# Scan of an RWKV-7 layer: keys and values turned to time-major order by quadrants of 64 rows with a 64-column identity

## The chip, the cores and the metric

The kernel is one program on one core of a Trainium2 chip. The metric is the device time of one execution in microseconds (us). TensorE multiplies, VectorE (DVE), ScalarE (ACT) and GpSimd (POOL) work element by element, SyncE (SP) issues most DMA transfers. Matmul results land in PSUM, eight banks of 128 partitions x 512 fp32. The engines run on their own and wait for each other by semaphores.

## What is computed

Two two-layer transformer blocks in a row: differential attention and SwiGLU, then an RWKV-7 time mixer and a mixture of experts; after that MLA with retention, a conv-FFN, gated linear attention and again a conv-FFN. The model width is 1024, the sequence 256 tokens (272 with 16 meta tokens in the first block), all in fp32. The change lies in the RWKV-7 mixer, whose core is a recurrence over time, run forward and in reverse, with 16 heads of 64 channels:

```python
def _wkv7_step(S, inp):
    r, w, k, v, kk, a = inp
    sa = jnp.einsum('bhvk,bhk->bhv', S, kk)
    S = S * w[:, :, None, :] - sa[..., None] * (kk * a)[:, :, None, :] + v[..., None] * k[:, :, None, :]
    y = jnp.einsum('bhvk,bhk->bhv', S, r)
    return S, y
...
    _, y_fwd = lax.scan(_wkv7_step, S0, (r_t, tm(decay[0]), tm(kd[0]), v_t, kk_t, tm(a[0])))
    _, y_bwd = lax.scan(_wkv7_step, S0, (r_t, tm(decay[1]), tm(kd[1]), v_t, kk_t, tm(a[1])), reverse=True)
    y = jnp.swapaxes(y_fwd + y_bwd, 0, 1)
```

## The kernel before

Each engine has its own program, written as Python functions in stages: attention, ffn, project, scan, out, router, experts, even, conv, odd, conv. Activations are channel-major: 8 tiles of 128 channels (i = 0 to 7) by time. A tile holds two heads, head p = 0 in partitions 0 to 63 and p = 1 in 64 to 127.

**The scan.** The recurrence is cut into chunks of C = 64 time steps. Direction 0 has a first chunk of C0 = 16 and four of 64, direction 1 has four of 64: nine units (n, ci). The state of direction 0 lies in the buffer that the traces call `ring`, that of direction 1 in `arena`. scan_pe, scan_act and scan_dve each hold a generator `steps(n)` for a direction and `bonus()` for side work. The function `streams` runs them in turn, one step of direction 0, one of direction 1, one of the bonus work, in the same pattern on each engine. So the order on each engine is fixed. Direction 0 leads by some steps; a warm-up of matmuls (L591) fills a gap ahead of direction 1.

**One unit on TensorE.** In order: G, the products of keys with queries within the chunk, for each half of the tiles (q = 0, 1) 16 pairs of 64x64 by 128 (L1425); after the half q = 0 the values are turned to time-major order (Vt, L1434); then Ut (L1440), 64x64 by 64; then both key tensors are turned (BKt, L1447). After that come up to five levels lv of an inverse by doubling: T (L1454), Y (L1463) and X (L1469), 64x64 by 32 each. Then Z (L1475 and, with the state, L1483), N (L1489), the new state S (L1507) and the output y (L1500, L1515). `for i, p in HEADS` goes over tiles 0, 4, 1, 5, 2, 6, 3, 7 with p = 0 and 1 in each. The stationary operand comes first in `e.matmul(out, stationary, moving)`. `own(p)` is the partition half of head p. `part(j, i)` is the half j XOR (i // 4), so that tiles 0 to 3 and 4 to 7 land in opposite halves. So consecutive matmuls of L1440 go to four quadrants of the array in turn.

**Turning.** A transposition is a matmul with the window of 64 time steps as stationary operand and an identity as moving operand. Before, it takes a whole tile: 128 rows by 64 columns against the 128x128 identity `con("ident")`, with both heads next to each other in 128 output columns. Two tiles in turn use the two column halves of the array (TILES).

**Evictions.** ScalarE copies Vt to d.NV with two instructions (L1588), each 64 partitions by 512, scaled by a mask of real rows, and BKt to d.BKt in one (L1595, 128x1024). N is copied by the same kind of pair (L1612) from two banks of four blocks. VectorE masks G (L1706) and fills Y and X by predicated copies (L1713, L1720, L1728, L1732). TensorE waits for Vt before Z and for BKt before S.

**PSUM.** `psum.take(key, n)` hands out banks in turn; for n = 2 it takes an even bank and the next, skipping an odd one. A new holder waits until the old one is evicted.

**The identities.** `sn("id2")` is a 128x64 constant that already lies in SBUF with the scan's constants: two 64x64 identities, one above the other. After the scan, the weight stream goes on: the transfer of the block that begins with "rw_o" waits for the last y of direction 0 (L3580).

Of the kernel before, what the change touches and what calls it, by code (L numbers as in the profile page):

```python
# [416 lines left out]
def build(nc, x_d, ws_d, par_d, con_d, dis_d, scn_d, rel_d, ow_d, moe_d, pos_d, out_d):  # L417
    fp32, i32, u32, f32r = mybir.dt.float32, mybir.dt.int32, mybir.dt.uint32, mybir.dt.float32r
    ALU, ACT, AX = mybir.AluOpType, mybir.ActivationFunctionType, mybir.AxisListType
    MUL, ADD, SUB, MAXO, MINO = ALU.mult, ALU.add, ALU.subtract, ALU.max, ALU.min  # L420
    ctx = ExitStack()
    with ctx:
# [38 lines left out]
        PS = ps_t[:, :, :]  # L461
# [4 lines left out]
        def con(n):  # L466
            return con_t[:, cc[n][0]:cc[n][0] + cc[n][1]]
# [21 lines left out]
        pe, dv, ac, po = (Signal(sem(f"s_{n}_done")) for n in ("pe", "dve", "act", "pool"))  # L489
# [8 lines left out]
        psum = Banks()  # L498
# [585 lines left out]
        Rr, Kr, KK, Vr, Yb = (at(i * AB, 8, T0) for i in range(5))  # L1084
# [187 lines left out]
        def sn(name):  # L1272
            return scn[:, sc[name][0]:sc[name][0] + sc[name][1]]
# [33 lines left out]
        HEADS = [(i + 4 * x, p) for i in range(4) for x in range(2) for p in range(2)]  # L1307
        STRAIGHT = [(i, p) for i in range(8) for p in range(2)]
        SAME = [(i, p) for i, p in HEADS if i // 4 != p]
        OTHER = [(i, p) for i, p in HEADS if i // 4 == p]  # L1310
        TILES = [i + 4 * x for i in range(4) for x in range(2)]

        def own(p, n=64):
            return slice(64 * p, 64 * p + n)

        def part(j, i, n=64):
            return own(j ^ (i // 4), n)
# [7 lines left out]
        def bank(b, i):  # L1325
            return b + i // 4

        def col(i, n=64):
            return slice(64 * (i % 4), 64 * (i % 4) + n)
# [58 lines left out]
        def window(d, j, i, c0):  # L1388
            a = j * AB + i * T0 + c0
            return d.flat[:, a:a + 64]  # L1390

        def scan_pe(w, e):
            w.wait_ge(ac["project"], IN_SCN)

            def steps(n):
                d = dirs[n]
                for hf in range(2):
                    for name, src in (("w2", HW), ("a2", HA)):
                        for i in range(4):
                            b, free = psum.take((name, n, hf, i))  # L1400
# [11 lines left out]
                for ci, (c0, cn) in enumerate(d.chunks):  # L1412
                    u = (n, ci)
                    cs = slice(c0, c0 + cn)

                    for q in range(2):
                        b, free = psum.take(("G", *u, q), 2)
                        w.wait_ge(*free)
                        for i, p in HEADS:
                            if i // 2 % 2 == q:  # L1420
                                x = 128 * (g_slot(i, p) % 4)
                                for j in range(2):
                                    out = PS[part(j, i), b + p, x:x + 2 * C].rearrange("s (r t) -> s r t", r=2)
                                    if cn == C:
                                        last = e.matmul(out, window(d, j, i, c0)[own(p)], d.AR[own(p), :, i, cs], start=True, stop=True)  # L1425
                                    else:
                                        last = e.matmul(out[:, 0, 0:cn], window(d, j, i, c0)[own(p)], d.AR[own(p), 0, i, cs], start=True, stop=True)
                        last.then_inc(*pe.on("G", *u, q))
                        if q == 0:
                            b, free = psum.take(("Vt", *u))  # L1430
                            w.wait_ge(*free)
                            for i in TILES:
                                x = 128 * (i % 4)
                                last = e.matmul(PS[part(1, i), b, x:x + 128], Vr[:, i, c0:c0 + 64], con("ident"), start=True, stop=True)  # L1434
                            last.then_inc(*pe.on("Vt", *u))
                        yield
                    b, free = psum.take(("Ut", *u), 2)
# [4 lines left out]
                    b, free = psum.take(("BKt", *u), 2)  # L1442
                    w.wait_ge(*free)
                    for j in range(2):
                        for i in TILES:
                            x = 128 * (i % 4)
                            last = e.matmul(PS[part(j, i), bank(b, i), x:x + 128], window(d, j, i, c0), con("ident"), start=True, stop=True)  # L1447
                    last.then_inc(*pe.on("BKt", *u))
                    yield
                    for lv in range(1, levels(cn)):  # L1450
# [96 lines left out]
        def scan_act(w, e):  # L1547
            w.wait_ge(IN_SCN, IN_PAR)

            def steps(n):  # L1550
# [32 lines left out]
                for ci, (c0, cn) in enumerate(d.chunks):  # L1583
                    u = (n, ci)
                    w.wait_ge(pe["Vt", *u])
                    real = sn("rows")[:, int(cn < C):int(cn < C) + 1]
                    for x in range(2):
                        e.activation(d.NV[own(1 - x), 8 * x:8 * x + 8, :].rearrange("q i t -> q (i t)"), PS[own(1 - x), psum["Vt", *u], :], ACT.Identity, scale=real[own(1 - x)]).then_inc(*ac.on())  # L1588
                    ac.mark("Vt", *u)
                    psum.gone["Vt", *u] = [ac.now()]  # L1590
                    yield
                    yield
                    w.wait_ge(pe["BKt", *u])
                    b = psum["BKt", *u]
                    e.activation(d.BKt.rearrange("q (x i) p t -> q x (i p t)", x=2), PS[:, b:b + 2, :], ACT.Copy).then_inc(*ac.on("BKt", *u))  # L1595
                    psum.gone["BKt", *u] = [ac.now()]
                    yield
                    for lv in range(1, levels(cn)):
                        w.wait_ge(pe["T", *u, lv])
                        b = psum["T", *u, lv]  # L1600
                        e.activation(side(d.T.rearrange("q (x i) t -> q x (i t)", x=2), lv, d.y_side), PS[:, b:b + 2, 0:128].rearrange("q x (i m) -> q x i m", m=2 ** lv), ACT.Copy).then_inc(*ac.on("T", *u, lv))
                        psum.gone["T", *u, lv] = [ac.now()]
                        yield
                        yield
                    w.wait_ge(pe["Z", *u])
                    e.activation(pairs(d.Z), eights(psum["Z", *u]), ACT.Copy).then_inc(*ac.on("Z", *u))
                    psum.gone["Z", *u] = [ac.now()]
                    yield
                    w.wait_ge(pe["N", *u])
                    b = psum["N", *u]  # L1610
                    for x in range(2):
                        e.activation(d.NV[own(x), 8 * x:8 * x + 8, :].rearrange("q (i p) t -> q p i t", p=2), PS[own(x), b:b + 2, 0:256].rearrange("q p (i t) -> q p i t", i=4), ACT.Identity, scale=real[own(x)]).then_inc(*ac.on())  # L1612
                    ac.mark("N", *u)
                    psum.gone["N", *u] = [ac.now()]
                    yield
                    if ci < d.last:
                        identity(ci + 1)
                        yield
                    if cn < C:
                        continue  # L1620
                    if y_first(n, c0):
                        w.wait_ge(pe["y", *u])
                        e.activation(pairs(Yb[:, :, c0:c0 + cn]), eights(psum["y", *u], cn), ACT.Copy).then_inc(*ac.on("y", c0))
                        psum.gone["y", *u] = [ac.now()]
                    yield
# [2043 lines left out]
```

## Time and profile before

| | |
|---|---|
| median of 3 runs | 2608.56 us (2607.54 to 2610.41) |
| span of the profiled execution | 2600.0 us |
| median less span (start, end, spread) | 8.56 us |
| instructions on all engines | 54,588 |
| TensorE matmul rows | 23,472, busy 2505.0 us (96%) |
| VectorE | busy 1998.4 us (77%) |
| ScalarE | busy 1537.2 us (59%) |
| the scan | about 559 to 795 us of the span |

The profile is of one execution. Its own time is given as the span, from the first to the last instruction; the runs' times also hold what lies around it. A row names the line, the engine, the operation, output<-input by the program's names, partitions x elements, and how many. TensorE has two kinds of rows, PE (matmul) and PEld (weight load). One fp32 matmul of the code shows as two matmul rows and two weight loads. "issue" is time in which an engine waited for nothing that the profile shows. PEclk is the clock that TensorE was granted, as a share of 2.4 GHz.

### The profile page before, as it was taken

To read this page: it belongs to the slowest core of one execution; us is meant where nothing else is said; L and a number is where in the kernel's file an instruction comes from. 1 tells how busy PE (TensorE), PEld (TensorE's weight loads), DVE (VectorE), ACT (ScalarE), POOL (GpSimd) and SP (SyncE) were. 2 spreads that over 40 slices of the span, in tenths; PEclk is the share of its full clock that TensorE was granted. 3 is DMA by queue.
4 is the path that set the end of the run, shared out by engine and by line. 5 is a ranking of instruction groups with operands and counts; after the bars stand their busy time and mean duration, and the time that the engine had idled before them with its cause. 6 is when DMAs were issued, how large, how long until landed. Compare 5 with 4: busy or idle time off the path is not lost.

```text
span 2600.0 us, 54588 instructions
## 1 busy us (share of the span) xinstructions
PE 2505.0 (96%) x23472; PEld 2331.7 (90%) x23472; DVE 1998.4 (77%) x3066; ACT 1537.2 (59%) x2510; POOL 51.9 (2%) x57
## 2 busy tenths in 40 slices
PE   8999999989999999999999999999898899999999
PEld 8779998868887899999999999999897799998999
DVE  5555547775544799999999999999877788675884
ACT  4435434464432677777777777777666566564663
POOL 0001100000000000000000000000003000000000
PEclk9999999978999999999999999999999999998999
DMA  6223452300003599999999999999732255541453
GB/s 246 73 74 122 178 190 100 107 1 4 20 4 115 206 376 337 367 340 368 341 366 335 372 337 370 335 373 345 287 139 105 78 192 191 188 173 50 171 181 128
DMA packets 83257, 538.46 MB, mean 207 GB/s; under 512 B 9488, under 2 KB 9616, under 8 KB 38976
## 3 DMA queue, kind: packets, MB, share of 16 engines
q1 hardware_dynamic: 82368, 530.68, 55.2%
q8 instruction: 186, 3.05, 0.5%
q0 software_dynamic: 640, 4.22, 0.4%
q14 instruction: 63, 0.52, 0.1%
HBM read 533.81 MB, written 1.05 MB: 206 GB/s over the span
## 4 chain that ended last, share of the span: by engine, by line
PE 87%; DVE 7%; ACT 4%; issue 1%; DMA 1%; DVEq 0%; SPq 0%; PEldq 0%; ACTq 0%
PE ps L576 23%; PE ps L577 23%; PE ps L578 23%; PE ps L1469 2%; DVE sl L534 2%; PE ps L591 1%; PE ps L582 1%; PE ps L2000 1%; PE ps L1463 1%; PE ps L1447 1%; PE ps L1454 1%; DMA ring<-ws_d 1%; PE ps L2145 1%; PE ps L1425 1%; PE ps L819 1%
## 5 line engine op out<-in xcount | busy, mean ns | idle before, releaser
L2227 DVE TENSOR_TENSOR sl<-ring,sh 128x1024 fp32r<-128x1024 f32 x613 | 718.1, 1219 | 13.5 <-ACT sh L2185 10.6
L2185 ACT ACTIVATE sh<-ring 128x1024 fp32r<-128x1024 f32 x613 | 609.0, 1061 | 1.3 <-DVE xl L2070 1.3
L576 PE MATMUL ps<-sh,xh 128*128 128x256 f32 (+2 forms) x2012 | 568.0, 282 | 2.1 <-DVE sl L534 1.2
L578 PE MATMUL ps<-sh,xl 128*128 128x256 f32 (+2 forms) x2012 | 567.5, 282 | 0.0
L577 PE MATMUL ps<-sl,xh 128*128 128x256 f32 (+2 forms) x2012 | 567.0, 282 | 0.0
L576 PE MATMUL ps<-xh,sh 128*128 128x256 f32 (+2 forms) x1856 | 538.5, 290 | 22.8 <-DVE sl L534 12.7
L577 PE MATMUL ps<-xl,sh 128*128 128x256 f32 (+2 forms) x1856 | 531.2, 286 | 0.0
L578 PE MATMUL ps<-xh,sl 128*128 128x256 f32 (+2 forms) x1856 | 529.0, 285 | 0.0
L534 DVE TENSOR_TENSOR sl<-ring,sh 128x1024 fp32r<-128x1024 f32 (+1 forms) x341 | 401.0, 1201 | 74.6 <-ACT sh L527 74.3
L527 ACT ACTIVATE sh<-ring 128x1024 fp32r<-128x1024 f32 (+1 forms) x341 | 338.8, 1021 | 111.2 <-PE ps L578 102.8
L576 PEld LDWEIGHTS ps<-sh,xh 128*128 128x128 f32 x2012 | 377.8, 188 | 11.8 <-DVE sl L534 1.6
L577 PEld LDWEIGHTS ps<-sl,xh 128*128 128x128 f32 x2012 | 377.8, 188 | 8.9
L576 PEld LDWEIGHTS ps<-xh,sh 128*128 128x128 f32 (+1 forms) x1856 | 353.3, 190 | 32.6 <-DVE sl L534 12.2
L578 PEld LDWEIGHTS ps<-sh,xl 128*128 128x128 f32 x2012 | 377.8, 188 | 0.3
L578 PEld LDWEIGHTS ps<-xh,sl 128*128 128x128 f32 (+1 forms) x1856 | 354.2, 191 | 0.0
L577 PEld LDWEIGHTS ps<-xl,sh 128*128 128x128 f32 (+1 forms) x1856 | 353.6, 191 | 0.6
L2199 ACT ACTIVATE arena_moe<-ps 128x128 f32<-128x128 f32 x224 | 62.3, 278 | 245.1 <-PE ps L578 244.9
L576 PE MATMUL ps<-sh,moe_h 128*128 128x512 f32 x336 | 145.8, 434 | 1.9 <-DVE kept_l L2232 1.9
L577 PE MATMUL ps<-sl,moe_h 128*128 128x512 f32 x336 | 131.9, 393 | 0.0
L578 PE MATMUL ps<-sh,moe_l 128*128 128x512 f32 x336 | 131.8, 392 | 0.0
L578 PE MATMUL ps<-conv_h,sl 128*128 128x256 f32 x352 | 99.3, 282 | 0.0
L577 PE MATMUL ps<-conv_l,sh 128*128 128x256 f32 x352 | 98.6, 280 | 0.0
(555 smaller groups left out, 3861.1 us busy)
## 6 DMA issues: line engine op xcount, KB each, us to landing
ring<-ws_d SPq DMA_DIRECT2D x229, 1024.0 KB, 7.2
ring<-ws_d SPq DMA_DIRECT2D x80, 1536.0 KB, 6.4
ring<-ws_d SPq DMA_DIRECT2D x225, 512.0 KB, 6.5
ring<-ws_d SPq DMA_DIRECT2D x24, 1408.0 KB, 6.0
ring<-ws_d SPq DMA_DIRECT2D x4, 1256.0 KB, 5.4
ring<-ws_d SPq DMA_DIRECT2D x2, 1088.0 KB, 5.0
scan_t<-scn_d POOLq DMA_DIRECT2D x1, 1844.0 KB, 7.5
ring<-ws_d SPq DMA_DIRECT2D x1, 1248.0 KB, 5.6
```

Source lines behind the costliest of these rows:

```text
L527: e.activation(sh[slot_of[bi]][:, c], ring[:, bi % RING, c], ACT.Copy).then_inc(*ac.on("high", bi, p))
L534: e.tensor_tensor(sl[s][:, c], ring[:, bi % RING, c], f32(sh[s][:, c]), SUB).then_inc(*dv.on("low", bi, p))
L576: e.matmul(out, ah, bh, start=start, stop=False)
L577: e.matmul(out, ah, bl, start=False, stop=False)
L578: return e.matmul(out, al, bh, start=False, stop=stop)
L582: return e.transpose(out, in_, con("ident")[0:k, 0:k])
L591: e.matmul(PS[:, b, 0:256], con("o1024"), con_t[:, WARM:WARM + 256], start=True, stop=True)
L819: e.matmul(PS[:, b, 0:256], v, aT[h % 2][0:kn, kt, :], start=kt == 0, stop=False)
L1469: last = e.matmul(spread(PS[own(p), b:b + 2, :], lv)[:, i], d.T[own(p, cn), i, :], side(d.X[own(p, cn), i, :], lv, d.x_side), start=True, ...
L2185: e.activation(out, raw(u)[:, a:z], ACT.Copy).then_inc(*af.on("high", u, i))
L2199: e.activation(sg_few[u % 2][:, 0, :], PS[:, u % 2, 0:128], ACT.Sigmoid).then_inc(*af.on("sigmoid", u))
L2227: e.tensor_tensor(l, raw(u)[:, a:z], f32(h), SUB).then_inc(s_fd if i < 2 else s_fp, 1)
```

## The change

Values: the 8 matmuls of 128x64 by 128 become 16 of 64x64 by 64, one for each head, with the half of the 64-column identity that lies on the head's partitions. Their output now takes two PSUM banks, one for each p, of which 256 columns each are used; before it was one bank of 512. Keys: the 16 matmuls of the two key tensors become 32 of the same small form, in the same two banks but ordered by head. ScalarE's copies read and write the new order; their sizes stay as they were. TILES goes.

```diff
--- before.py
+++ after.py
@@ -1308,7 +1308,6 @@
         STRAIGHT = [(i, p) for i in range(8) for p in range(2)]
         SAME = [(i, p) for i, p in HEADS if i // 4 != p]
         OTHER = [(i, p) for i, p in HEADS if i // 4 == p]
-        TILES = [i + 4 * x for i in range(4) for x in range(2)]
 
         def own(p, n=64):
             return slice(64 * p, 64 * p + n)
@@ -1427,11 +1426,10 @@
                                         last = e.matmul(out[:, 0, 0:cn], window(d, j, i, c0)[own(p)], d.AR[own(p), 0, i, cs], start=True, stop=True)
                         last.then_inc(*pe.on("G", *u, q))
                         if q == 0:
-                            b, free = psum.take(("Vt", *u))
+                            b, free = psum.take(("Vt", *u), 2)
                             w.wait_ge(*free)
-                            for i in TILES:
-                                x = 128 * (i % 4)
-                                last = e.matmul(PS[part(1, i), b, x:x + 128], Vr[:, i, c0:c0 + 64], con("ident"), start=True, stop=True)
+                            for i, p in HEADS:
+                                last = e.matmul(PS[part(1, i), b + p, col(i)], Vr[own(p), i, c0:c0 + 64], sn("id2")[own(p)], start=True, stop=True)
                             last.then_inc(*pe.on("Vt", *u))
                         yield
                     b, free = psum.take(("Ut", *u), 2)
@@ -1442,9 +1440,8 @@
                     b, free = psum.take(("BKt", *u), 2)
                     w.wait_ge(*free)
                     for j in range(2):
-                        for i in TILES:
-                            x = 128 * (i % 4)
-                            last = e.matmul(PS[part(j, i), bank(b, i), x:x + 128], window(d, j, i, c0), con("ident"), start=True, stop=True)
+                        for i, p in HEADS:
+                            last = e.matmul(PS[part(j, i), b + p, 64 * i:64 * i + 64], window(d, j, i, c0)[own(p)], sn("id2")[own(p)], start=True, stop=True)
                     last.then_inc(*pe.on("BKt", *u))
                     yield
                     for lv in range(1, levels(cn)):
@@ -1584,15 +1581,16 @@
                     u = (n, ci)
                     w.wait_ge(pe["Vt", *u])
                     real = sn("rows")[:, int(cn < C):int(cn < C) + 1]
+                    b = psum["Vt", *u]
                     for x in range(2):
-                        e.activation(d.NV[own(1 - x), 8 * x:8 * x + 8, :].rearrange("q i t -> q (i t)"), PS[own(1 - x), psum["Vt", *u], :], ACT.Identity, scale=real[own(1 - x)]).then_inc(*ac.on())
+                        e.activation(d.NV[own(1 - x), 8 * x:8 * x + 8, :].rearrange("q (i p) t -> q p i t", p=2), PS[own(1 - x), b:b + 2, 0:256].rearrange("q p (i t) -> q p i t", i=4), ACT.Identity, scale=real[own(1 - x)]).then_inc(*ac.on())
                     ac.mark("Vt", *u)
                     psum.gone["Vt", *u] = [ac.now()]
                     yield
                     yield
                     w.wait_ge(pe["BKt", *u])
                     b = psum["BKt", *u]
-                    e.activation(d.BKt.rearrange("q (x i) p t -> q x (i p t)", x=2), PS[:, b:b + 2, :], ACT.Copy).then_inc(*ac.on("BKt", *u))
+                    e.activation(d.BKt.rearrange("q i p t -> q p i t"), PS[:, b:b + 2, :].rearrange("q p (i t) -> q p i t", i=8), ACT.Copy).then_inc(*ac.on("BKt", *u))
                     psum.gone["BKt", *u] = [ac.now()]
                     yield
                     for lv in range(1, levels(cn)):
```

## Rows read from the trace of the kernel before

**Rows 1.** The page: busy time by engine, and the instruction queue (packets, MB, share).
```profile
PE 2505.0 (96%) x23472; PEld 2331.7 (90%) x23472; DVE 1998.4 (77%) x3066; ACT 1537.2 (59%) x2510; POOL 51.9 (2%) x57
...
q8 instruction: 186, 3.05, 0.5%
```

**Rows 2.** Stretches: busy us (instructions) of each engine, granted clock, DMA share, GB/s.
```profile
559.00:586.00 27.00, 20.86 (x279) 16.66 (x277) 22.49 (x32) 14.71 (x23) 0.00 (x0) 0.75 0.01 2
586.00:600.00 14.00, 11.10 (x311) 9.40 (x311) 7.83 (x14) 6.84 (x12) 0.00 (x0) 0.88 0.01 4
601.00:615.00 14.00, 14.00 (x309) 11.97 (x310) 4.89 (x10) 5.13 (x10) 0.00 (x0) 0.51 0.01 4
615.00:767.00 152.00, 144.60 (x5100) 129.58 (x5092) 81.52 (x148) 59.50 (x109) 0.53 (x1) 1.00 0.04 11
670.00:751.00 81.00, 75.35 (x2826) 69.54 (x2820) 39.86 (x71) 30.07 (x53) 0.53 (x1) 1.00 0.06 17
1200.00:1500.00 300.00, 300.00 (x2192) 282.04 (x2191) 291.61 (x420) 226.72 (x348) 0.00 (x0) 1.00 0.96 356
```

**Rows 3.** Chain of waits, 713 to 752 us: start, duration, engine and line, count.
```profile
713.34 0.59 PE ps L1447 x8
713.93 0.48 issue
714.41 1.53 PE ps L1447 x24
...
718.09 0.59 PE ps L1454 x25
718.68 0.47 PE ps L1463 x32
...
721.85 0.59 PE ps L1454 x25
...
724.48 0.95 issue
725.43 0.83 PE ps L1469 x22
...
729.17 0.97 PE ps L1507 x25
...
730.75 0.93 PE ps L1469 x32
...
746.46 0.88 issue
```

**Rows 4.** DMA queues, 670 to 751 us: packets, MB, share of 16 engines.
```profile
q8 instruction: 22, 0.36, 1.9%
```

**Rows 5.** Order of time on TensorE, 618 to 650 us: start, us, instruction, count.
```profile
621.04 0.69 PE L1440 MATMUL ps<-scan_t 64*64 64x64 f32 x32
621.66 1.97 PE L1447 MATMUL ps<-con,scan_t 128*64 128x128 f32 x32
...
641.48 1.09 PE L1434 MATMUL ps<-con,arena 128*64 128x128 f32 x16
```

**Rows 6.** Chain of waits, 555 to 625 us, lines of the opening.
```profile
568.47 2.97 PE ps L1447 x31
...
587.29 1.05 PE ps L1434 x16
...
594.48 3.60 PE ps L1447 x31
...
609.04 1.01 PE ps L1463 x32
```

**Rows 7.** Order of time on ScalarE, 567 to 573 us; idle time before in brackets.
```profile
571.46 1.02 ACT L1595 ACTIVATE ring<-ps 128x1024 f32<-128x1024 f32 x1 [0.65 <-PE ps L1447]
```

**Rows 8.** Groups of the scan by form: count, busy us, mean ns, idle before.
```profile
L1588 ACT ACTIVATE ring<-ps,scan_t 64x512 f32<-64x512 f32 x10 | 6.8, 682 | 7.4 <-PE ps L1434 7.3
...
L1612 ACT ACTIVATE ring<-ps,scan_t 64x512 f32<-64x512 f32 x8 | 5.5, 682 | 6.9 <-PE ps L1489 6.8
```

## Prediction

> **What bounds the kernel now.** The first view is the page's head [rows 1]: TensorE is busy for 96% of the span of 2600.0 us. The change touches only the scan, so the second view is the table of stretches [rows 2]. It splits the scan in two. From 559 to 615 us the recurrences of the two directions start: TensorE, ScalarE and VectorE wait for one another, and TensorE's granted clock is at its lower level (1.2 GHz) for part of the time: 0.75, 0.88 and 0.51. From 615 to 767 us both directions run level by level, the clock is at its full 2.4 GHz and TensorE is busy for 144.60 of 152.00 us. One would say that it is TensorE-bound, and that whatever shortens a matmul shortens the kernel.
>
> The third view, the chain of waits, says otherwise [rows 3]. In 713 to 751 us it is nearly all TensorE, but with holes put down to "issue", as 0.48, 0.95 and 0.88 us. Nothing on another engine ends them. They fall inside a group of like matmuls: the one at 713.93 cuts the 32 of L1447 into 8 and 24, which have no wait between them. Work resumes at 714.41, 718.09, 721.85, 725.43 and 729.17 us, so 3.68, 3.76, 3.58 and 3.74 us apart, mean 3.69, whatever the line.
>
> The fourth view, the DMA queues, has the same period [rows 4]: from 670 to 751 us queue q8, of kind "instruction", moved 22 packets, one each 81.0/22 = 3.68 us. In that stretch TensorE ran 2826 matmuls and 2820 weight loads [rows 2], 5646/22 = 257 for each packet. On the page q8 has 186 packets in all and TensorE 46,944 such instructions [rows 1], 252 for each. So q8 brings TensorE its instructions in packets of 3.05 MB/186 = 16.4 KB; from 670 to 751 us TensorE eats them as fast as they come and stands idle in between. The bound there is the number of instructions, at 81.0 us/5646 = 14.3 ns each, and not the matmuls' time. In all of 615 to 767 us it is 152.0/10,192 = 14.9 ns each, so within 4% of that rate.
>
> **The change, part by part.** (1) TensorE's time. The keys and values of one chunk and direction (a unit; there are nine) take 8 matmuls for Vt and 16 for BKt, with a stationary operand of 128x64 and 128 moving columns. The trace shows each fp32 matmul as two matmul rows and two weight loads: from first start to last end 16 rows take 1.09 us, 32 take 1.97 us and L1440's 32 take 0.69 us [rows 5]. The next group starts 0.07 us before that end (621.04 + 0.69 against 621.66), so they hold the engine for 1.02, 1.90 and 0.62 us. After the change there are 32 and 64 rows of 64x64 by 64. The nearest row is L1440, with the same order over heads, the same quadrants (rows by p, columns by i // 4), the same two banks and the same 64 columns: 32 rows in 0.62 us, with a change of array shape before and after it. L1463, with its neighbours in the same shape, takes 0.47 us for 32 rows [rows 3]. I take 0.5 us for Vt and 1.0 us for BKt, since they now stand among matmuls of their own shape. That is 1.02 + 1.90 - 1.5 = 1.4 us less TensorE time in each unit, 12.8 us in nine; with 0.62 for each 32 it would be 1.06 us, 9.5 in all.
>
> On this the Trainium skill has two rules. The page "TensorEngine Tiling (Array Packing)", section "Tiling Modes", says that a 64x64 mode has four independent tiles and that a change of mode drains the array. The second agrees with the longer L1440, and both promise the gain in full, which is rival B below. The page "TensorE: Matmul & The Clock Gate", section "Wait — 56ns, not 53.3ns?", has a floor of about 25 ns from one matmul to the next however few the columns. By it the 96 rows of a unit would take 2.4 us and the gain would be 0.5 us. The trace has 0.62 us/32 = 19 ns for quadrant matmuls, so it does not bear the floor out here.
>
> (2) TensorE's instructions. Each added matmul brings two more matmul rows and two more weight loads. Vt goes from 32 to 64 instructions and BKt from 64 to 128: 96 more in each unit, 864 in the kernel, 864/257 = 3.4 more packets. This is what decides.
>
> Two of the nine units have their first Vt and BKt before 615 us (three of the four are in rows 6), so seven Vt and seven BKt lie from 615 to 767 us. That is 672 more instructions: 10,192 + 672 = 10,864. At the supply's 14.35 ns they need 155.9 us, 3.9 us more than the 152.0 of now. TensorE's own need falls by 7 x 1.4 = 9.8 us to 142 us, which is less than 155.9 and so buys nothing: it turns into longer holes. The price has bounds. With the shortest distance of two restarts, 3.58 us for 257 instructions or 13.9 ns, it is 151.3 us, 0.7 us less than now. With today's mean of this stretch, 14.9 ns, it is 162.0 us, a loss of 10.0 us. I take 14.35, as the stretch that has the holes is the one where supply alone sets the pace.
>
> (3) The opening, before 615 us. There supply is no bound: TensorE ran 622 instructions in the 14 us from 586 to 600 us [rows 2], 22.5 ns each, and waits for others. Three of the transposes are on the chain [rows 6]. BKt of the first unit ends at 571.44, then ScalarE evicts it (L1595, at 571.46), and only then starts direction 1's exponentials. ScalarE had been idle for 0.65 us there [rows 7], and BKt, 2.97 us now and at the lower clock in part, comes down to about half of that, so it is ready before ScalarE is: 0.65 us is gained. Vt of direction 1's first unit (587.29, 1.05 us) is waited for by L1588: 0.5 us. BKt of the same unit takes 3.60 us, most of it at the lower clock, ahead of L1595; at half speed L1463 takes 1.01 us for 32 rows [rows 6], so 64 rows want 1.8 to 2.0 us: 1.6 us, from 1.0 (all of it at the full clock before and after) to 2.6 (lower clock before, full after). Sum 2.75 us, bounds 2.0 and 3.8. What is late next is the queue of ScalarE (L1595, L1636, L1601), which moves along with BKt. The first unit's Vt is not in the chain: nothing. The stretch from 601 to 615 us at clock 0.51 has no transpose in it.
>
> (4) ScalarE's evictions. Vt's two now read two banks of four blocks each in place of 512 contiguous columns. L1612 is exactly the new form and takes 682 ns against 682 of L1588 [rows 8]: nothing. BKt's still moves 128x1024, 1.02 us now [rows 7]; its output goes in runs of 64, as that of L1612. Nothing, with a bound of 0.1 us for either sign.
>
> (5) PSUM. Vt takes two banks in place of one. The next request (G of the other half, two banks, aligned) skipped the odd one anyway, unless a one-bank request of the bonus work came between. No new wait is expected; the bound is one eviction's 0.7 us now and then, in a stretch where supply has TensorE waiting anyway. No DMA, no queue and no other wait is moved.
>
> (6) After the scan all is shifted: the transfer for the next projection waits for its last y (sp_program, L3580), and everything later for that. The code behind starts 96 instructions off the old packet borders. From 1200 to 1500 us TensorE ran 4383 instructions in 300 us, 68 ns each [rows 2], so packet borders cost nothing there.
>
> Sum: +3.9 - 2.75 = +1.15 us on the span of 2600.0 us. The median shown is 8.56 us above that span, which I keep: 2608.56 + 1.15 = 2609.7. The coverage by holes is never perfect (a wait for ScalarE adds to a packet's time where it doesn't fall in with a hole), so I round up to 2610.
>
> **The rivals.** A, the forecast: supply takes the gain, 2610. Its own range goes from 13.9 ns with 3.8 us of opening (-0.7 - 3.8 = -4.5) to 14.6 ns with 2.0 us (158.6 us, +6.6 - 2.0 = +4.6): 2604 to 2613.
>
> B: TensorE's time decides. For it: 144.60 of 152.00 us are busy, the chain is TensorE's, and outside 670 to 751 us holes are few: 144.60 - 75.35 = 69.3 of 71 us are busy. Against it: the restarts at a fixed 3.7 us. It would need the next packet to be asked for earlier when TensorE eats faster. It gives -12.8 us, with some of it lost to waits for VectorE and ScalarE: 2596 to 2600.
>
> C, the other side: the supply doesn't keep 14.35 ns for the new mix. The packets bunch: a unit's Ut and BKt become 192 instructions in a row in about 1.5 us, and other stretches are slow in instructions (L1515, L1425, the wait for L1612), so these go at TensorE's pace and the dense ones at the supply's, and both lose. That is today's 14.9 ns kept in spite of shorter matmuls: 162.0 us, +10.0 - 2.75 = +7.3 us, 2616. For it speaks that 615 to 767 us has 14.9 and not 14.35 today. It ends over the 0.2% line from 14.75 ns on (10,864 x 14.75 = 160.2 us, +8.2 - 2.75 = +5.5).
>
> D: the clock. From 601 to 615 us the grant is 0.51 while TensorE is busy for all 14.00 us [rows 2]; what went before is a stretch with waits at 0.88. These 14 us cost some 7. If the shift of 3 us or the thinner work before it moves that fall away, the gain is up to 7 us, 2603; if another such stretch comes, as holes grow, the loss is the same, 2617.
>
> E: the change doesn't do what it says, the quadrants not overlapping: L1469, whose blocks lie on the diagonal alone, needs 0.93 us for 32 rows [rows 3], and 96 rows at that pace 2.8 us, today's time. Then the opening gains nothing and supply still adds 3.9: 2612.5.
>
> **How the numbers follow.** A 0.50, B 0.12, C 0.20, D 0.13 (0.07 on the slow side, 0.06 on the fast), E 0.05. A measurement of this kernel tells about 0.2%, 5.2 us, from no change. Faster by more: B and most of D's fast side, 0.17. Slower by more: C and D's slow side, 0.27. Within: A and E, 0.56. The range leaves out B and the far ends of C and D: 2602 to 2618.
>
> **What the profile of after would show.** Right: rows of Vt and BKt at 0.5 and 1.0 us where they are not cut by a hole; q8 packets spaced at 3.6 to 3.8 us all through 615 to 770 us, 10,864/257 = 42 in place of 40, and 189 or 190 in all; more and longer "issue" holes, TensorE not busy for some 20 us of that stretch against 7.4; the scan's end within 3 us of now. Wrong: q8 packets nearer than 3.4 us (B), or a q8 mean above 3.8 us (C); a clock under 1.00 after 615 us, or over 0.6 from 601 to 615 (D); 32 rows of Vt in 0.9 us (E). If L1595 takes over 1.1 us, step 4 was wrong.

## The result, and the profile after

| | before | after |
|---|---|---|
| median of 6 runs each, taken in turn on one chip | 2608.05 us (2602.03 to 2612.46) | 2618.88 us (2615.99 to 2622.20) |
| ratio, 95% interval | | 1.0046 (1.0032 to 1.0061) |
| profiled execution, span | 2600.0 us | 2619.9 us |
| mean granted clock of TensorE over the run, mean of runs | 0.977 (109 runs, this study) | 0.971 (6 runs) |

The change makes the kernel 0.46% slower, 10.8 us. The forecast was 2610, its range ended at 2618.

The page of after, first the busy time by engine, then the instruction queue:

```profile
PE 2509.8 (96%) x23904; PEld 2332.2 (89%) x23904; DVE 1998.0 (76%) x3066; ACT 1536.9 (59%) x2510; POOL 51.8 (2%) x57
...
q8 instruction: 190, 3.11, 0.5%
```

There are 864 more TensorE instructions (47,808 for 46,944) and 190 packets for 186 [rows 1], as counted ahead. The stretches of after have the columns of [rows 2]; the last is new:

```profile
559.00:586.00 27.00, 18.59 (x325) 14.91 (x324) 22.55 (x33) 17.45 (x29) 0.00 (x0) 0.71 0.01 2
586.00:600.00 14.00, 11.71 (x345) 9.87 (x348) 10.92 (x16) 5.54 (x9) 0.00 (x0) 0.87 0.01 4
601.00:615.00 14.00, 13.75 (x282) 11.77 (x283) 4.53 (x9) 5.35 (x11) 0.00 (x0) 0.50 0.02 4
615.00:767.00 152.00, 131.56 (x5147) 120.01 (x5148) 76.45 (x139) 56.69 (x103) 0.53 (x1) 0.97 0.04 11
670.00:751.00 81.00, 67.38 (x2765) 62.28 (x2764) 39.73 (x72) 26.15 (x47) 0.53 (x1) 0.98 0.05 17
767.00:795.00 28.00, 25.96 (x573) 20.40 (x571) 8.62 (x16) 5.02 (x11) 0.00 (x0) 0.64 0.01 3
```

The same last stretch of before:

```profile
767.00:795.00 28.00, 25.61 (x750) 20.34 (x746) 8.79 (x19) 7.84 (x16) 0.00 (x0) 1.00 0.01 4
```

Two things are to be seen. From 615 to 767 us TensorE is busy for 131.56 us, not 144.60: it has less to do and does not get on faster. From 767 to 795 us it is busy as before, but the grant is 0.64, not 1.00, and it does 573 matmuls where it did 750. Its clock is at 1.2 GHz from 775.0 to 802.3 us.

The chain of waits of after shows both (start, duration, engine and line; L1444 is the new BKt, L1451, L1460 and L1466 are the old L1454, L1463 and L1469; L1535 and L1536 are the bonus work of the old L1538 and L1539):

```profile
719.60 1.01 issue
721.46 0.91 PE ps L1444 x64
722.68 1.85 issue
...
746.27 0.91 issue
749.58 1.17 issue
...
771.05 1.52 issue
773.00 0.93 PE ps L1466 x31
775.34 1.86 PE ps L1451 x64
777.20 1.20 PE ps L1535 x2
778.40 1.20 PE ps L1536 x2
779.61 1.01 PE ps L1460 x32
```

The holes put down to "issue" are longer than in [rows 3], up to 1.85 us where the longest was 0.95. Behind the last BKt comes one of 1.52 us. After 775 us every group takes nearly twice its time: L1460 1.01 us, where before's L1463 has 0.60 in the same stretch, L1535 1.20 where L1538 has 0.66. In before:

```profile
776.52 0.60 PE ps L1454 x32
...
779.38 0.66 PE ps L1538 x2
780.04 0.65 PE ps L1539 x2
780.69 0.60 PE ps L1463 x32
```

The scan's stages are split here by where groups start: G of direction 0, G of direction 1, G of the second unit of direction 0, the last G, the centering behind the scan. The low clock is the time at 1.2 GHz in that stage.

| us | before | after | after, second profile | low clock before / after / second |
|---|---|---|---|---|
| ahead of the scan (it starts at) | 560.0 | 563.7 | 563.2 | 34.1 / 41.0 / 41.0 |
| opening | 54.5 | 53.1 | 55.6 | 30.2 / 36.3 / 42.8 |
| main part | 142.4 | 150.2 | 147.1 | 0.5 / 8.1 / 8.4 |
| tail | 38.6 | 52.1 | 51.8 | 0 / 27.3 / 27.3 |
| behind the scan | 1804.5 | 1800.9 | 1808.0 | 42.8 / 42.7 / 56.4 |

The 19.9 us between the two spans are +3.7 ahead of the scan, -1.4, +7.8, +13.5 and -3.6 behind it. The parts outside the scan have the same code and move too: over the fifteen profiles of this study the scan starts at 558.4 to 566.0 us, and the part behind it takes 1800.8 to 1811.8 us. The tail is the one term that stands clear of this.

### The profile page after: what moved, and what is told of

Read it like the earlier page. It is cut to its first block, busy times and chain, and to the rows that moved or that the text cites. A ratio compares the mean times of both kernels' runs of the same rounds, so it can differ in the third digit from the quotient of the medians.

```text
span 2619.9 us, 55454 instructions
## 1 busy us (share of the span) xinstructions
PE 2509.8 (96%) x23904; PEld 2332.2 (89%) x23904; DVE 1998.0 (76%) x3066; ACT 1536.9 (59%) x2510; POOL 51.8 (2%) x57
## 3 DMA queue, kind: packets, MB, share of 16 engines
HBM read 533.81 MB, written 1.05 MB: 204 GB/s over the span
## 4 chain that ended last, share of the span: by engine, by line
PE 84%; DVE 9%; ACT 4%; issue 2%; DMA 1%; DVEq 0%; SPq 0%; PEldq 0%; ACTq 0%
PE ps L576 23%; PE ps L577 22%; PE ps L578 22%; DVE sl L534 2%; PE ps L1466 2%; PE ps L591 1%; PE ps L582 1%; PE ps L1998 1%; PE ps L1460 1%; PE ps L1451 1%; PE ps L819 1%; PE ps L1424 1%; ACT sh L527 1%; DMA ring<-ws_d 1%; PE ps L2143 1%
## 5 line engine op out<-in xcount | busy, mean ns | idle before, releaser
L2225 DVE TENSOR_TENSOR sl<-ring,sh 128x1024 fp32r<-128x1024 f32 x613 | 718.2, 1220 | 13.2 <-ACT sh L2183 10.5
L576 PEld LDWEIGHTS ps<-sh,xh 128*128 128x128 f32 x2012 | 377.7, 188 | 11.7 <-DVE sl L534 1.5
L576 PE MATMUL ps<-sh,moe_h 128*128 128x512 f32 x336 | 145.8, 434 | 1.9 <-DVE kept_l L2230 1.9
L576 PE MATMUL ps<-conv_h,sh 128*128 128x256 f32 x352 | 98.4, 279 | 0.8 <-DVE sl L534 0.8
```

Source lines behind the costliest of these rows:

```text
L576: e.matmul(out, ah, bh, start=start, stop=False)
L2225: e.tensor_tensor(l, raw(u)[:, a:z], f32(h), SUB).then_inc(s_fd if i < 2 else s_fp, 1)
```

## The experiments

All runs below are medians, with the kernel before run in turn on the same chip. Main part and tail are read as in the table above, from one profile each. The distance of packets is the mean from start to start of the packets of q8 that start in the main part. The main part of one profile is uncertain by some 3 us: nops96, which turned out to be a copy of before, has 145.8 for 142.4.

**after_again.** No edit: the changed kernel a second time.

> The changed kernel once more, beside the others. Theory S (instruction supply): in the profile the q8 packets stand 3.7 to 3.8 us apart from 622 us to the end of the units, 672 more instructions at 14.4 to 14.7 ns, +8 us there, -1 to -3 us in the opening. Theory D (clock) explains the rest of +10.8 us: lower-clock stretches of 20 to 27 us between the last unit's transposes and the end of the scan, worth 10 to 13 us; if the profile has no such stretch, the total is +5 to +7 us.

2619.73 us (2604.72 to 2632.61, 12 runs), ratio 1.0042 (1.0022 to 1.0063). The tail has the same 27.3 us at the low clock. The runs are spread widely and the spread goes with the clock: 2604.72 us at a mean grant of 0.977, 2632.61 us at 0.968. So the loss repeats, and the clock is in it.

**bkt_only and vt_only.** One half of the change each.

> Only the keys (BKt) by quadrants, the values as before: 576 more TensorE instructions, 448 of them in the supply-bound part. S: +448 x 14.4 ns = +6.5 us, less 1.5 us in the opening, +5 us. TensorE-time theory: 9 x 0.9 = -8 us. If the clock drops at the scan's end here too, up to 10 us more.

> Only the values (Vt) by quadrants, the keys as before: 288 more instructions, 224 of them in the supply-bound part. S: +3.2 us less 0.5 us in the opening, +2.7 us. TensorE-time theory: 9 x 0.5 = -4.5 us. Clock: less than with the keys.

```diff
 # bkt_only: BKt as after, Vt as before
-for i, p in HEADS:
-    last = e.matmul(PS[part(1, i), b + p, col(i)], Vr[own(p), i, c0:c0 + 64], sn("id2")[own(p)], ...)
+for i in TILES:
+    last = e.matmul(PS[part(1, i), b, x:x + 128], Vr[:, i, c0:c0 + 64], con("ident"), ...)
```

bkt_only: 2627.32 us (6 runs), ratio 1.0065 (1.0042 to 1.0087), main part 156.2 with 18.9 us at the low clock, tail 53.1 with 30.7. vt_only: 2604.68 us (12 runs), ratio 0.9992 (0.9977 to 1.0006), main part 143.0, tail 39.7 with none. The whole loss is BKt's. That bkt_only stands some 8 us above the changed kernel goes with the clock of its six runs: put to one grant both are at 2608 us (table of runs below). Vt alone costs nothing and gains nothing that can be told.

**nops96.** To the kernel before, 96 no-operations on TensorE in each unit.

> The kernel before with 96 TensorE no-operations after each unit's key transposes: as many instructions as the change adds (864), and no matmul touched. S: +672 x 14.4 ns = +9.7 us from 615 us on, and no gain in the opening, +10 us or a little more. TensorE-time theory: no-operations cost next to nothing, 0 to +2 us. Clock: TensorE's matmuls stay as thick as before in each unit but holes grow, so if holes alone bring the clock down, it falls here too.

2607.69 us, ratio 1.0004 (0.9991 to 1.0018), but with 186 packets: the no-operations left no instruction in the program. It tests nothing of supply, and stands as a control.

**half_keys and few_keys.** The kernel before with less TensorE time in BKt. In half_keys the moving operand has 64 of the 128 columns, so head 1 of each tile gets the turned keys of head 0; the count of instructions is kept. In few_keys tiles 4 to 7 are not turned but get those of tiles 0 to 3, which takes away 32 of BKt's 64 instructions. In both, ScalarE's copy of BKt reads each block twice, so that its output stays as large.

```diff
 # half_keys
-    last = e.matmul(PS[part(j, i), bank(b, i), x:x + 128], window(d, j, i, c0), con("ident"), ...)
+    last = e.matmul(PS[part(j, i), bank(b, i), x:x + 64], window(d, j, i, c0), con("ident")[:, 0:64], ...)
 # few_keys
-for i in TILES:
+for i in range(4):
```

> The kernel before with key transposes of 128x64 by 64 columns in place of 128: head 1 of each tile is left out of the transposes and gets head 0's keys. As many instructions as before, TensorE time of the key transposes about halved. TensorE-time theory: 9 x 0.8 = -7 us. S: the stretch from 615 us stays at 14.4 to 14.9 ns per instruction, gain only in the opening and the loose part, -2 to -4 us. D: thinner TensorE work alone brings the clock down at the scan's end, +8 to +14 us, with no instruction added.

> The kernel before with key transposes of tiles 0 to 3 alone (8 matmuls a unit in place of 16, 128x64 by 128 as before); tiles 4 to 7 are left out and get the keys of tiles 0 to 3. TensorE time of the key transposes is halved as in half_keys, but here with 32 instructions less a unit. S: 224 fewer in the supply-bound part, 3.2 us less than half_keys there, so -6 to -7 us on the kernel before. TensorE-time theory: the same as half_keys, -3.5 us.

Stretch 615 to 767 us of half_keys, columns as in [rows 2]:

```profile
615.00:767.00 152.00, 140.42 (x5102) 125.68 (x5100) 81.42 (x149) 59.71 (x109) 0.53 (x1) 1.00 0.04 11
```

The busy time falls from 144.60 to 140.42 us and the stretch holds the same 10,202 instructions (10,192 in [rows 2]); the main part is 142.6 us for 142.4, the total 2603.67 us, ratio 0.9991 (0.9980 to 1.0003). So in the main part shorter matmuls alone buy nothing that one profile can tell (the 4.2 us taken away are little more than the 3 us of nops96), which fits a pace set by the supply. The clock does not fall in the tail either, though BKt's matmuls are thin. few_keys: 2603.41 us, ratio 0.9987 (0.9972 to 1.0002), main part 144.2. Fewer instructions bring no more than shorter ones. The supply is not the only bound of the main part: its packets come 3.93 us apart for 3.82 in half_keys, and it is no faster. Part of that is its clock, which is low for 6.4 us of its main part, for 0.8 in half_keys.

**paired.** Keys interleaved by chunk in memory, so that one 128-column stationary operand holds both tensors: G becomes 64x128 and BKt 128x128 matmuls. That makes 192 matmul and weight-load rows in a full unit into 96, and what is computed stays the same; VectorE gets eight more, smaller operations, and ScalarE's decay factors wait for the keys.

```diff
-for j in range(2):
-    last = e.matmul(PS[part(j, i), bank(b, i), x:x + 128], window(d, j, i, c0), con("ident"), ...)
+last = e.matmul(PS[:, bank(b, i), x:x + 128], both(d, i, c0), con("ident"), ...)
```

> Fewer instructions, same results: the two key tensors lie next to each other by chunk, so that G takes 16 matmuls of 64x128 by 128 a unit in place of 32 of 64x64, and BKt 8 of 128x128 in place of 16 of 128x64. 96 TensorE instructions less in each of the eight full units, about as many as the change adds, with TensorE's streaming time near that of before; VectorE has 8 more small instructions in the opening, ScalarE none. S: 670 instructions less in the supply-bound part, -9.6 us until TensorE's own time takes over (it was busy for 144.6 of 152 us), so -5 to -7 us there, +1 us in the opening: -4 to -6 us in all, q8 at 182 or 183 packets. TensorE-time theory: 0 to +2 us. D: the clock stays up (all of the array in use more often).

Page and stretch of paired:

```profile
q8 instruction: 183, 3.00, 0.5%
...
615.00:767.00 152.00, 145.12 (x4689) 132.11 (x4686) 81.59 (x148) 58.12 (x105) 0.53 (x1) 0.98 0.04 11
```

2607.11 us, ratio 0.9996 (0.9981 to 1.0012). The gain of 4 to 6 us that I expected is not there. The packets now come 4.04 us apart on average in the main part (3.81 before), so supply no longer sets the pace; TensorE is busy for 145.12 us, as before. The reading that fits half_keys, few_keys and paired is that supply and TensorE's own work are level in the kernel before, so that taking from either alone gives nothing. It is argued, from one profile each.

**fill_after, wide and fill_tail.** The changed kernel with TensorE given thicker work. fill_after puts three idle matmuls of 128x128 by 256 ahead of each BKt, fill_tail ahead of the last unit's BKt of each direction only. wide lets 24 of the 32 matmuls of BKt have 128 moving columns (the extra 64 are overwritten by the next), with not one instruction more.

```diff
 # fill_tail (fill_after: in every unit)
+for _ in range(3 if ci == d.last else 0):
+    e.matmul(PS[:, b, 0:256], con("o1024"), con_t[:, WARM:WARM + 256], start=True, stop=True)
 # wide
-    last = e.matmul(PS[part(j, i), b + p, 64 * i:64 * i + 64], ..., sn("id2")[own(p)], ...)
+    last = e.matmul(PS[part(j, i), b + p, 64 * i:64 * i + wide], ..., eye, ...)
```

> The changed kernel with three filler matmuls of 128x128 by 256 ahead of each unit's key transposes (12 instructions and about 1.3 us of TensorE a unit, in the bank that the transposes then overwrite). Theory D (the clock falls because the quadrant form keeps too little of the array at work): the clock stays at 1.00 from 620 us to the scan's end, the tail is back at 39 us, and only the supply's price is left, +2 to +6 us on the kernel before. If the clock has nothing to do with what the matmuls fill, the 1.3 us a unit come on top: +11 to +20 us.

> The changed kernel with 128 moving columns in place of 64 for 24 of a unit's 32 key transposes (the surplus columns are overwritten by the next one): the same instructions as in the changed kernel, and TensorE time of the kernel before. S alone: as the changed kernel, +10 us, since holes take up the time. D, if streaming columns in quadrants is what counts: clock back to 1.00, +2 to +6 us. D, if rows of the array in use count (64 of 128): clock falls as in the changed kernel.

> The changed kernel with three filler matmuls of 128x128 by 256 ahead of the key transposes of the last unit of each direction only. D, with the fall decided by what stands just ahead of it: the lower-clock stretch of 27 us in the tail goes, the scan's tail is back to 39 to 41 us from 52, median +0 to +4 us on the kernel before. D, with the fall built up over all the units: the tail stays at 52 us and the median at +11 us or above.

The stretch that fell in after, here in fill_tail, then wide:

```profile
767.00:795.00 28.00, 27.05 (x829) 21.81 (x822) 11.93 (x22) 8.33 (x17) 0.00 (x0) 1.00 0.02 4
```

```profile
767.00:795.00 28.00, 26.16 (x834) 21.16 (x826) 12.14 (x23) 8.67 (x17) 0.00 (x0) 1.00 0.02 4
```

In all three the grant is 1.00 and the tail 40.3 or 40.4 us, for 52.1: 12 us are back, in the profiled execution. The totals gain less. fill_after 2616.04 us, ratio 1.0042 (1.0028 to 1.0056); wide 2613.30, 1.0037 (1.0019 to 1.0054); fill_tail 2614.22, 1.0024 (1.0011 to 1.0038). A filler of three takes 1.49 us in fill_tail, so six in fill_tail cost 3 us and the 27 of fill_after 13 us at the full clock if nothing hides them. The main part stays at 150.5 us in wide and in fill_tail and is 153.2 us in fill_after. So the fillers and the wider form bring back the tail, but the intervals of all three overlap with that of the changed kernel (1.0032 to 1.0061): that the total gains by them is not shown.

**vt_open.** vt_only with 12 filler matmuls, meant for the opening, to raise its clock. So that they can run while TensorE waits, the wait for T and X stands behind them. In the profile eight of them run in the opening and four at 623 and 631 us, in the main part.

```diff
+for _ in range(2 if u in ((0, 0), (1, 0)) else 0):
+    e.matmul(PS[:, b, 0:256], con("o1024"), con_t[:, WARM:WARM + 256], start=True, stop=True)
```

> Only the values by quadrants (as vt_only), and 12 filler matmuls of 128x128 by 256 in the waits of the first unit of each direction. If these lift the clock from 597 to 620 us, the opening loses most of its 30 to 40 us at the lower level, worth up to 10 us: -5 to -10 us. If not, the fillers cost up to 5 us where nothing hides them: 0 to +3 us.

2615.06 us, ratio 1.0030 (1.0013 to 1.0046). The opening still has 33.3 us at the low clock (vt_only 35.3) and is 57.0 us long for 54.6. The fillers buy no clock there. The 10 us above vt_only are not all theirs: in the two profiles the opening is 2.4 us longer and the main part 1.4, but the part behind the scan, whose code is the same, 7.4, with 59.7 us at the low clock for 45.9.

**keep_last and thin_tail.** Which units bring the fall? keep_last is the changed kernel with the old BKt in the last unit of each direction; thin_tail is the kernel before with the new BKt in these two units alone.

```diff
 # keep_last (thin_tail: the condition turned round)
+for i in (TILES if ci == d.last else []):
+    x = 128 * (i % 4)
+    last = e.matmul(PS[part(j, i), bank(b, i), x:x + 128], window(d, j, i, c0), con("ident"), ...)
-for i, p in HEADS:
+for i, p in ([] if ci == d.last else HEADS):
```

> The changed kernel, but the keys of the last unit of each direction are turned as before the change: 16 matmuls with 128 columns. The seven other units keep the quadrants; 128 TensorE instructions fewer than the changed kernel, so 189 or 190 packets. Theory L (the thin BKt of the last two units makes the clock fall near 775 us): the clock stays at 1.00 from 767 to 795 us, the way from the last G to the end of the scan is 38 to 41 us against 52, and the time is that of the changed kernel less 8 to 13 us: 2606 to 2611. Theory M (the fall comes from what went before, holes and thin work of the whole main part): the clock falls in the tail all the same, the tail takes 50 us or more, and the time is 2616 to 2622.

> The kernel before, but with the quadrant form of BKt in the last unit of each direction alone: 128 TensorE instructions more than before, 187 packets. Theory L (the last two units' thin BKt is enough): a fall of some 27 us in the tail at clock 1.2 GHz, tail 50 to 53 us, time 2617 to 2621. Theory M (it needs the holes of the main part, of which this kernel has few, about 9 to 13 us): no fall, tail 38 to 40 us, time 2605 to 2610.

Two stretches of keep_last:

```profile
615.00:767.00 152.00, 135.79 (x5046) 124.00 (x5042) 74.48 (x137) 56.37 (x102) 0.53 (x1) 0.92 0.04 11
767.00:795.00 28.00, 27.05 (x725) 20.72 (x717) 11.90 (x23) 8.08 (x17) 0.00 (x0) 1.00 0.01 4
```

and of thin_tail:

```profile
767.00:795.00 28.00, 27.35 (x771) 20.98 (x769) 9.58 (x20) 7.46 (x17) 0.00 (x0) 1.00 0.02 4
```

keep_last: 2613.76 us (2605.97 to 2616.82), ratio 1.0020 (1.0005 to 1.0034), tail 39.7 us with none at the low clock; but in its main part the clock fell for 20.5 us from 625.0 us on (grant 0.92), and that part took 153.6 us, 26.6 of them at the low clock. thin_tail: 2609.71 us (2602.45 to 2622.23), ratio 1.0017 (1.0000 to 1.0034), no fall in the profile; its slowest runs have the lowest clock (2622.23 us at 0.971, 2602.45 us at 0.980). So, as far as one profile each can tell, the fall in the tail goes with the new form in the last two units, but that form does not force it, which is neither theory in full. The ratios share the loss out: 0.17% for the two units alone, 0.20% for the seven others, 0.42 to 0.46% for all nine. The first two are barely clear of nothing.

**The hole behind the last BKt.** One more thing sets the kernels apart. In the three profiles with the long fall an "issue" hole starts within 0.5 us of the end of the last BKt and 2 to 4 us ahead of the fall: 1.52 us in after, 1.52 in after_again, 1.51 in bkt_only. In thin_tail it is

```profile
764.30 1.43 issue
```

and in wide 1.17 us, in vt_open 0.27, in fill_tail 0.18, in the other eight none; none of these falls. So where a hole of the supply lies goes along with the fall as well as the form of the matmuls does, and fillers or other counts of instructions move that too. No run holds one of the two and changes the other. A hole alone does not bring a long fall: after has one of 1.85 us at 722.68 and is low for only 3.4 us behind it, from 730.6 us.

**Time and clock, run by run.** Each run lists its span and the mean grant of TensorE's clock. Over 258 runs of 14 kernels, each against its own kernel's mean, the time goes up by 2.0 us for each 0.001 of mean grant lost, and what is left scatters by 2.6 us. A thousandth of 2610 us is 2.6 us of full clock, or 5.2 us spent at the half level. Put to a grant of 0.977 with that slope:

| kernel | runs | mean us | mean grant | us at 0.977 |
|---|---|---|---|---|
| before | 109 | 2607.6 | 0.9767 | 2607.0 |
| after and after_again | 18 | 2619.3 | 0.9714 | 2608 |
| bkt_only | 6 | 2624.8 | 0.9685 | 2608 |
| vt_only | 12 | 2604.5 | 0.9777 | 2606 |
| nops96 | 12 | 2607.8 | 0.9766 | 2607 |
| keep_last | 12 | 2612.4 | 0.9738 | 2606 |
| thin_tail | 12 | 2610.7 | 0.9757 | 2608 |
| fill_tail | 12 | 2614.6 | 0.9735 | 2608 |
| fill_after | 6 | 2617.4 | 0.9757 | 2615 |
| vt_open | 12 | 2614.9 | 0.9762 | 2613 |
| wide | 11 | 2616.0 | 0.9749 | 2612 |
| half_keys | 12 | 2603.7 | 0.9761 | 2602 |
| few_keys | 12 | 2604.7 | 0.9762 | 2603 |
| paired | 12 | 2607.9 | 0.9760 | 2606 |

At equal clock the changed kernel stands 1 us behind the one before. The other 10 or 11 us go with 0.005 of mean grant. This is a correlation, and fill_tail shows its limit. Its profile has no fall in the tail, and the grant of that same execution is still 0.974. The time at the low clock lies elsewhere: 51.2 us ahead of the scan, where before has 34.1 with the same code, and 8.6 in the main part, where before has 0.5. So a kernel's mean grant holds more than what its change does.

## Why the prediction was wrong

**What bounds the kernel: right in part.** half_keys takes 4 us of TensorE time out of the stretch with the number of instructions kept, and the main part does not move. But paired, with fewer instructions and the same TensorE time, does not move it either, so the number of instructions is not the only bound.

**(1) TensorE's time: right.** In the order of time of after, the new groups at full clock (start, us, instruction, count):

```profile
650.92 1.11 PE L1444 MATMUL ps<-scan_t 64*64 64x64 f32 x62
...
667.48 0.64 PE L1432 MATMUL ps<-scan_t,arena 64*64 64x64 f32 x32
```

The chain gives L1444 0.91 us for 64 rows (721.46), 1.0 was taken. L1432's next group starts 0.46 us after it (667.94), 0.5 was taken. Rival E is out.

**(2) The supply: right in kind, its size open.** +3.9 us was worked out, with 42 packets in place of 40 and some 20 us without work. TensorE is not busy for 20.4 us of 615 to 767 us. The main part has 40 packets for 38, on average 3.80 us apart for 3.81. It grew by 7.8 us, with 7.6 us more at the low clock. At half speed these cost 3.8 us at most, less where they fall in with holes: 4 us or more are left. In the second profile it is +4.7 and 7.9 us of low clock, 0.8 left. wide and fill_tail, with the same number of instructions or nearly, have +8.1 with 2.4 and with 8.1 us more of low clock. But nops96, the same program as before, has +3.4 with 1.3 more, vt_only, with a third of the added instructions, +0.6 with 1.8, and keep_last +11.2 with 26.1, less than half speed would make it. Whether the supply's price is 1 or 7 us can't be told from these profiles.

Rival B is out: the packets come no closer. (Its sign, packets nearer than 3.4 us, could not have told: single ones are 3.33 us apart in before as in after.) Rival C is not out. Its mechanism was today's mean rate kept in spite of shorter matmuls, and 3.80, 3.81 and 3.81 us for a packet in after, wide and fill_tail are today's 3.81; the forecast's 14.35 ns are 3.69 us for 257 instructions, and after_again comes nearest with 3.72. What speaks against C's +7.3 us in all is the 1 us that is left at equal clock.

**(3) The opening: too high.** -2.75 us was taken with bounds of 2.0 and 3.8. It is -1.4 and +1.1 us in the two profiles, each with more low clock than before (6.1 and 12.5 us). BKt of the first unit was no longer waited for, as ScalarE came to it straight from L1562 (start, us, instruction):

```profile
573.12 2.13 ACT L1562 ACTIVATE scan_t<-arena,scan_t,par 128x272 f32<-128x272 f32 x4
575.16 1.00 ACT L1593 ACTIVATE ring<-ps 128x1024 f32<-128x1024 f32 x1
```

But this piece gained nothing: L1593 is released 11.5 us behind the start of the scan, as before, since L1402 ahead of it held the chain for 3.14 us in place of 2.44 of its old line, L1403. The other two did shorten:

```profile
590.96 0.52 PE ps L1432 x31
...
597.62 1.75 PE ps L1444 x62
```

Vt of direction 1 has 0.52 us in place of 1.05, its BKt 1.75 in place of 3.60, together 2.4 us for the 2.1 taken. Behind them 1.0 us went again at the low clock. The step failed in keeping the clock of [rows 2] for the rest: the grant was 0.71 in place of 0.75 for the first 27 us. How much of that is the change's doing is open: nops96, the code of before, has an opening of 55.4 us.

**(4) The evictions: right.** L1586, the old L1588, is at 682 ns and L1593 at 1.00 us, against 682 ns and 1.02 us [rows 7, 8]. **(5) PSUM and (6) behind the scan** show no new wait in the chains; behind the scan the time goes -3.6 and +3.5 us, one way in one profile and the other way in the other.

**Where it went wrong: rival D.** Its slow side said 2617 us, near what was measured, with a chance of 0.07. (C's 2616 us is as near, and no better borne out.) I took the fall at 601 us [rows 2] as a single stretch that may move, be spared or come twice, 7 us each, by chance. What the runs show is that the kernels with the new BKt have a lower grant: 0.9714 and 0.9685 for 0.9767, over 18, 6 and 109 runs. The three profiled kernels that have it in all nine units with nothing thicker beside it (after, after_again, bkt_only) have 27.3, 27.3 and 30.7 us at the low clock in the tail, and 13.5, 13.2 and 14.5 us more tail. Of the profiles of the others none has that. Shorter matmuls without more instructions (half_keys) don't bring it, nor do as many instructions with wider ones (wide). But half_keys differs in more than the number, as it also keeps 128 rows of the array, and wide has a shorter hole behind its last BKt. TensorE is idle for 20.4 us of 615 to 767 us in after and for 11.6 in half_keys, which keeps its clock, but for 18.8 in wide, which keeps it too: the idle share alone does not decide. What in the new BKt lowers the grant is not settled.

The step that failed is thus "a clock under 1.00 after 615 us" being priced as an accident beside the sum, where the runs show it as the main term: 13.5 us in the tail, and by the runs' grant 10 or 11 of the 11.7 us between the means. There was reason to ask for it: step (1) takes 12.8 us of work away, step (2) says that it turns into holes, and [rows 2] shows, from 559 to 615 us, this engine's clock low among holes. That it would fall did not follow from this, as wide and thin_tail show; that it was met within 2 us by a rival of 0.07, whose price of one fall was 7 us where the tail lost 13.5, is luck.

On the clock the Trainium skill ("TensorE: Matmul & The Clock Gate", "Part 1: The HAM clock gate") ties the lower level to an idle engine. The trace does not bear that out alone: the hole just ahead of the fall is 1.52 us, the longest of the main part 1.85 us, and from 767 to 795 us, with the clock low from 775.0 us on, TensorE is busy for 25.96 of 28 us.

## What to carry to other kernels

Where an engine waits for its own instructions, a form with more and shorter instructions turns its saving into holes. Ask at once what these holes do to the clock: it can cost more than the whole saving, in a stretch behind the change. And where two bounds may be level, as supply and TensorE's own time seem to be here, an experiment that relieves one of them shows nothing; paired took 768 instructions away and gained nothing. A term of 4 us needs more than one profile of each kernel: the main part of one and the same program came out at 142.4 and at 145.8 us.

## What the hardware showed that I had not expected

- Once low, the grant stayed low for 27.3 us in after, from 775.0 us, with TensorE busy for 25.96 of 28 us in quadrant matmuls. In before the same groups of L1454, L1463, L1469 and the bonus work ran there at a grant of 1.00 all through.
- The place of a fall is not fixed: 775 us in after, 774 in after_again, 781 in bkt_only, 625 in keep_last. One program's runs range from a mean grant of 0.967 to 0.979 and from 2604.72 to 2632.61 us (after_again). A difference of 0.4% can be a difference of clock alone, so the grant of each run is to be read beside its time.
- With three filler matmuls of 128x128 by 256 (1.49 us) ahead of the last BKt the tail stayed some 12 us shorter; with twelve in and behind the opening its low clock changed by 2 us.
- The packets of instructions come 3.72 to 3.81 us apart on average over the main part in before, after, after_again and vt_only, with 9604 to 10,216 instructions in it, and 4.04 us in paired, which has the fewest, 9004. In no variant is the mean under 3.72 us.
